# First projection of a sparse-attention layer as seven half-size products, with its bias copies re-queued, and a third row-sum buffer in sample attention

## The reference, cut to what matters

```python
def nsa_project(xn, w_in):                      # xn: tokens x 1024
    p = xn @ w_in                               # 1024 -> 1024 (q) + 6*256 (k/v of three branches) + 48 gates
    q  = p[..., :1024];  kv = p[..., 1024:2560]
    gates = sigmoid(p[..., 2560:])

def compress(x, w1, w2, pe):                    # per 32-row block, stride 16, over cached rows and new ones
    hid = einsum('id,ide->e', pe, w1) + sum_j einsum('nbigd,ide->nbge', xs[:, j:j + nc], w1r[j])
    return silu(hid) @ w2

def nsa_sample(...):                            # for each of the 8 sample sequences
    past = cache_kv[page_table]                 # paged rows, 4 pages of 128 per sequence
    kc, vc = compress(...)                      # compressed keys and values
    # three masked softmaxes with a relative bias: over compressed blocks, over selected
    # blocks, and over a window of 512; outputs are weighted by the gates and summed
```

## Time and profile before

| | |
|---|---|
| median of 3 executions | 2386.98 us (2385.87 to 2387.09) |
| the profiled execution: its own time | 2385.12 us |
| its span in the profile | 2383.4 us |
| TensorE busy | 2283.0 us (96% of the span) |
| VectorE, ScalarE, GpSimd busy | 1062.1, 565.0, 1114.8 us |
| moved by DMA | 197.14 MB, 83 GB/s on average |

### The profile page before, as it was taken

The page is one execution under the profiler, slowest core; times in us unless marked ns, Lnnn a source line. Parts: engine busy times, 40 slices in busy tenths (PEclk is TensorE's granted clock), DMA queues, the critical chain, the costliest instruction groups (busy, mean ns, idle before and its releaser), DMA issues. The chain is left out here.

```text
span 2383.4 us, 37660 instructions
## 1 busy us (share of the span) xinstructions
PE 2283.0 (96%) x14910; PEld 1705.0 (72%) x14910; DVE 1062.1 (45%) x1959; ACT 565.0 (24%) x1303; POOL 1114.8 (47%) x1004
## 2 busy tenths in 40 slices
PE   9999999889999999999999999999999999999997
PEld 7775444466777777767777778687776767777776
DVE  2112786445430242267986646463543153302422
ACT  1002666311000000136554323232420010000011
POOL 3331554255663465375665242342425466634653
PEclk9999999999999999999999999999999999999999
DMA  9723000742211222212222020110203112112211
GB/s 341 238 79 131 1 1 1 238 157 71 71 71 71 88 79 81 107 67 73 61 69 72 6 107 2 57 57 23 90 6 145 72 71 71 71 71 89 89 71 40
DMA packets 53144, 197.14 MB, mean 83 GB/s; under 512 B 15410, under 2 KB 26418, under 8 KB 36978
## 3 DMA queue, kind: packets, MB, share of 16 engines
q1 hardware_dynamic: 45778, 173.59, 20.3%
q0 software_dynamic: 3856, 15.61, 1.9%
q10 hardware_dynamic: 3344, 5.61, 1.1%
HBM read 170.86 MB, written 32.17 MB: 85 GB/s over the span
## 5 line engine op out<-in xcount | busy, mean ns | idle before, releaser
L1803 PE MATMUL ps<-xn,ring 128*128 128x288 f32 x768 | 198.9, 408 | 5.4 <-DVE xn L1906 3.2
L1803 PE MATMUL ps<-hid,ring 128*128 128x288 f32 x768 | 192.8, 406 | 0.0
L1803 PEld LDWEIGHTS ps<-xn,ring 128*128 128x128 f32 x768 | 145.6, 190 | 48.0 <-DVE xn L1906 5.9
L1803 PEld LDWEIGHTS ps<-hid,ring 128*128 128x128 f32 x768 | 145.9, 190 | 40.4 <-ACT p L1840 0.7
L1886 POOL TENSOR_TENSOR prod<-prod,rstd 128x1152 f32<-128x1152 f32 x32 | 83.8, 2620 | 179.7 <-DVE prod L1970 163.4
L1840 ACT ACTIVATE p<-ps 128x288 f32<-128x288 f32 x48 | 19.7, 410 | 597.4 <-PE ps L1803 597.4
L245 PE MATMUL ps<-xn,ring 128*128 128x288 f32 x576 | 140.1, 407 | 1.8 <-DMA ring<-in_w_nsa_in 1.8
L3215 PE MATMUL ps<-xn,ring 128*128 128x288 f32 x512 | 137.1, 415 | 3.6 <-PE ps L3284 3.6
L862 POOL TENSOR_SCALAR ring<-ring,fac 128x128 f32<-128x128 f32 (+2 forms) x96 | 92.6, 981 | 96.1 <-DVE fac L1098 96.1
L1803 PE MATMUL ps<-x_sum,wsum 128*128 128x288 f32 x512 | 130.6, 407 | 3.4 <-DVE x_sum L1910 1.9
L245 PEld LDWEIGHTS ps<-xn,ring 128*128 128x128 f32 x576 | 109.6, 190 | 32.2 <-DMA ring<-in_w_nsa_in 2.3
(11 more groups left out here) (503 smaller groups left out, 4800.8 us busy)
## 6 DMA issues: line engine op xcount, KB each, us to landing
ring<-in_w_mlp SPq DMA_DIRECT2D x64, 1024.0 KB, 4.8
ring<-in_w_gdn_in SPq DMA_DIRECT2D x16, 1024.0 KB, 4.8
ring<-in_w_nsa_in SPq DMA_DIRECT2D x9, 1024.0 KB, 15.8
ring<-in_w_gdn_z SPq DMA_DIRECT2D x8, 1024.0 KB, 4.9
x<-in_seq_state SPq DMA_DIRECT2D x4, 2048.0 KB, 8.4
out_seq_state<-x SPq DMA_DIRECT2D x4, 2048.0 KB, 10.9
ring<-in_w_gdn_out SPq DMA_DIRECT2D x8, 1024.0 KB, 5.7
out_win_old<-in_win_rows POOLq DMA_DIRECT2D x1, 8064.0 KB, 47.7
```

Source lines behind the costliest of these rows:

```text
L1803: mm = nc.tensor.matmul(S.ps[:, base + BANK[p], 0:HT], stationary(p, blk.units[pair // 4], pair % 4), moving(blk.kind, p, pair), start=pai ...
```

## The change

- Units 1 to 9 of the first projection are multiplied as seven products of half size. A unit is laid out as four quarters (`quadrants` instead of `units` in the host's preparation), each of 4 tiles; with the sums of weight quarters (`sum_weights`, 4 VectorE operations of 128x512 a unit) and of token blocks (`sums`, 4 of 128x1152 once) a unit takes 7 x 4 = 28 matmuls of the same shape in place of 32. ScalarE copies three products out of PSUM (`p1`, `p5`, `p6`) and one quarter of the result, VectorE makes the rest (`combine`, 5 operations of 128x288), and `project` scales as before, now in place in `S.qkv`. Unit 0 is multiplied as before (`first_unit`).
- The bias copies go out on SyncE's queue: `near_scratch` in four pieces behind the refills of units 4 to 7, `rows_scratch` in two behind units 8 and 9. They are read back only after the projection, since `toep` and `rowb` hold sums until then. The load of `w2` moves ahead of the refills.
- The token sums lie in the buffer of page set `u` = 2. So GpSimd loads sets 0 and 1 during the projection, and set 2 is loaded after it by three queues: SyncE one page of four, GpSimd one, ScalarE two.
- TensorE's order after the projection is first(0), first(1), gates, second(0), first(2), the transposes, second(1), first(3), second(2), second(3). The four fillers are gone.
- In the sample attention `rsum` has three buffers, `exp` of `n` waits for `combine` of `n - 3`, and the three fillers at `w == 4` are gone.

```diff
-            for u in (0, 2, 1):
-                if u == 2:
+            for u in range(2):
+                if u == 1:
                     pool.wait_ge(setup.summed, 1)
...
+            pool.wait_ge(d.product, 7 * (NB - 1))
+            late_pages(pool, 2, (1,), early_rows[1])
             pool.wait_ge(product, 2)
-            late_pages(pool, 1)
+            late_pages(pool, 3, (1, 3), late[1])
...
+            for n in range(1, NB):
+                base = 4 * (n % 2)
+                pe.wait_ge(d.loaded[n % SLOTS], 16 * (n // SLOTS + 1))
+                for p in PRODUCTS:
...
+                    if p == 2:
+                        pe.wait_ge(p1_read, n)
+                    elif p == 7:
+                        pe.wait_ge(p6_read, n)
+                    elif p == 3:
+                        pe.wait_ge(p5_read, n)
+                    if p in SUMMED:
+                        pe.wait_ge(w_summed, 4 * (n - 1) + SUMMED[p])
...
+                    for pair in range(4):
+                        mm = nc.tensor.matmul(S.ps[:, base + BANK[p], 0:HT], stationary(p, n, pair), moving7(p, pair),
+                                              start=pair == 0 and p in OPENS, stop=pair == 3, skip_group_check=True)
+                    mm.then_inc(d.product, 1)
...
+            def sum_weights(n):
+                slot, s2 = n % SLOTS, n % 2
+                dve.wait_ge(d.loaded[slot], 16 * (n // SLOTS + 1))
+                if n > 2:
+                    dve.wait_ge(d.product, 7 * (n - 2))
+                v.tensor_tensor(wsum[:, s2, 0], quad[:, slot, 2], quad[:, slot, 3], ALU.add).then_inc(w_summed, 1)
+                v.tensor_tensor(quad[:, slot, 2], quad[:, slot, 0], quad[:, slot, 2], ALU.subtract).then_inc(w_summed, 1)
...
+            project(0)
+            project(1)
+            for n in range(1, NB):
+                if n + 1 < NB:
+                    sum_weights(n + 1)
+                combine(n)
...
-        nmax, rsum, fac = sb("dnmax", [128, 2]), sb("drsum", [128, 2, 2]), sb("dfac", [128, 2])
+        nmax, rsum, fac = sb("dnmax", [128, 2]), sb("drsum", [128, 3, 2]), sb("dfac", [128, 2])
...
-                if w == 4:
-                    keep_busy(S, 3, TB)
...
-                if n >= 2:
-                    act.wait_ge(comb, n - 1)
+                if n >= 3:
+                    act.wait_ge(comb, n - 2)
                 a_.activation(sc[w % 3][:], sc[w % 3][:], ACT.Exp, bias=nmax[:, w % 2:w % 2 + 1],
-                              accum_out=rsum[:, n % 2, br:br + 1]).then_inc(prob, 1)
+                              accum_out=rsum[:, n % 3, br:br + 1]).then_inc(prob, 1)
```

More of the change, by code:

```diff
@@ L204, in dense_products @@
     iters = d.units // body
[L206 to L221, removed]
     def group(it, g):
-        if first_in is not None and it == 0 and g == 0:
-            return first_group()
         for ks in range(d.kslots):
@@ L262, in dense_products, with first_unit @@
         group(iters, g)
+def first_unit(pe, S, moving, scaled, first_in, first_mm):
+    nc = S.nc
+    for k in range(KD):
+        pe.wait_ge(*first_in[k // 2])
+        pe.wait_ge(scaled[k % 2], k // 2 + 1)
+        for m in range(2):
+            w = S.ring[:, 0, k * 256 + m * 128:k * 256 + m * 128 + 128]
+            x = moving(k)
+            for half in range(2):
+                mm = nc.tensor.matmul(S.pairs[:, m, half, :], w, x[:, half * HT:half * HT + HT], start=k == 0, stop=k == KD - 1)
+            if k == KD - 1:
+                mm.then_inc(first_mm, 1)
 def dense_chunks(eng, S, d, emit, after=None, ready=None):
@@ L468, in setup_vector @@
                 add_square(j)
+    sums(0)
     dve.wait_ge(u.line_mm, 1)
@@ new lines, in _ @@
+            setup_vector(dve, S, setup, sq, sums)
+            def project(c):
+                out = chunk(S.qkv, c)
+                raw = out
+                if c < 2:
+                    dve.wait_ge(first_mm, c + 1)
+                    raw = S.pairs[:, c]
+                v.scalar_tensor_tensor(out=out, in0=raw, scalar=DH ** -0.5 if c < 8 else 1.0,
+                                       in1=S.rstd[:, 1].rearrange("p (h t) -> p h t", h=2), op0=ALU.mult, op1=ALU.mult
+                                       ).then_inc(made, 1)
@@ new lines, in combine @@
+            def combine(n):
+                a, b, c, e = (S.ps[:, 4 * (n % 2) + k, 0:HT] for k in range(4))
+                after = lambda p: dve.wait_ge(d.product, 7 * (n - 1) + STEP[p])
+                dve.wait_ge(p1_read, n)
+                dve.wait_ge(p6_read, n)
+                if n > 1:
+                    dve.wait_ge(c12, n - 1)
+                v.tensor_tensor(u2, p1, p6, ALU.add).then_inc(u2_set, 1)
+                after(7)
+                if n > 1:
+                    dve.wait_ge(c21, n - 1)
+                v.tensor_tensor(u3, p1, b, ALU.add).then_inc(u3_set, 1)
+                dve.wait_ge(u3_set, n)
+                dve.wait_ge(p5_read, n)
+                v.tensor_tensor(prod(n)[:, 1, HT:T], u3, p5, ALU.add).then_inc(c22, 1)
+                after(4)
+                v.tensor_tensor(prod(n)[:, 1, 0:HT], u3, e, ALU.add).then_inc(c21, 1)
+                after(3)
+                dve.wait_ge(u2_set, n)
+                v.tensor_tensor(prod(n)[:, 0, HT:T], u2, c, ALU.add).then_inc(c12, 1)
+                dve.wait_ge(c11, n)
+                dve.wait_ge(c12, n)
+                dve.wait_ge(c21, n)
+                dve.wait_ge(c22, n)
+                project(2 * n)
+                project(2 * n + 1)
```

192 lines of the change are left out of this document (138 added, 54 removed).

## The result

| | before | after |
|---|---|---|
| median | 2387.03 us (2385.87 to 2389.47, 4 runs) | 2442.03 us (2439.54 to 2446.87, 4 runs) |
| ratio | | 1.0232, 95% interval 1.0219 to 1.0246 |
| profiled execution, its span | 2385.12, 2383.4 us | 2443.72, 2442.1 us |
| first compression product | 168.57 us | 231.00 us (forecast 149.0) |
| start of the prompt attention | 222.27 us | 287.44 us (forecast 204.0) |

The change made the kernel 2.3% slower. The forecast was 2359.3 us; what happened is the rival with a chance of 0.05, and more of it than that rival had priced.

The account below looks back on a forecast made before the run. TensorE's work was taken to bound the first projection, a pipeline across engines the sample attention. 18.2 + 9.5 = 27.7 us off the profiled 2385.1 gave 2357.4, as a median 2359.3 us; range 2354.3 to 2373.

Parts of the forecast that it names:

- Products: First projection, units 1 to 9: 13.58 us a unit, VectorE's sums hidden, compression starts at 149.0, 19.6 us less.
- A quarter took 60.3 / 4 = 15.1 us beside the other copies, and should take less alone.: SyncE's queue, units 5 to 9: each bias piece drains within 15.1 us, so refills stay ahead and cost nothing.
- the bias pieces hold up every refill: Rival, SyncE's queue, units 4 to 9: refills every 20.1 us, 2393.2 us, slower by 6; chance 0.05.
- Unit 4's weights: First projection: needed at 67.5 us, expected in time, cost taken as 0 with bounds 0 and 7.8 us.
- the first rival: First projection: unit 4's weights come late all the same, at 75.3 us, giving 2367.1 us; chance 0.14.
- The count by turns: Unit 4's weights: two queues with work instead of three, so a 34 us wait and arrival near 58 us.
- the count by bytes: Unit 4's weights: about 2.4 MB less beside them at 280 GB/s, 8.7 us, so arrival near 66.6 us.
- Behind unit 9: Compression to next stage: page loads bind by 3 us, stage ends at 204.0; 1.4 of the 19.6 us go here.
- The clock's share: Behind unit 9: 1 us added for a lower TensorE clock after 3 us of idleness.
- Sample attention: Exponential no longer waits for combine, loop takes about 6.0 instead of 6.69 us a sequence: 9.5 us less, lower bound 3.4.
- The 2.7 us for the fillers: Sample attention: with the fillers gone the next transposes come 2.7 us sooner, part of the 13.1 us upper bound.

Follow-up runs that it names:

- rows16_win4: Changed kernel with bias pieces cut across rows (all 16 heads each) and win_old's copy in four later parts: 2361.19 us, ratio 0.9888.
- rows16: Changed kernel with each bias piece cut out of the rows (all 16 heads) instead of out of the heads: 2377.25 us, ratio 0.9963.
- before_win4: Kernel before the change with win_old's copy in four parts behind halves of its page sets 0 and 2: 2387.83 us, ratio 1.0010.
- rsum3_alone: Kernel before the change with only the third row-sum buffer in the sample attention, fillers kept: 2382.41 us, ratio 0.9969.
- win4_busy: rows16_win4 with the old kernel's four filler groups put back ahead of the last compression set: 2367.05 us, ratio 0.9910.
- whole_sp: Changed kernel with the near copy as one DMA behind unit 4's weights and the row copy as one behind unit 9's, on SyncE's queue: 2393.95 us, ratio 1.0042.
- win4_strided: rows16_win4 with near pieces of four heads, each piece read from every fourth partition: 2366.85 us, ratio 0.9919.

## Why the prediction was wrong

**Products.** Right. In rows16_win4 the nine units run from 26.59 to 148.81 us, 13.58 us each, with no wait in between: VectorE's sums are hidden.

**"A quarter took 60.3 / 4 = 15.1 us beside the other copies, and should take less alone."** This is the step that failed. I divided a duration by the number of pieces and took the rate over. The whole copy reads 16 partitions, a piece as it was cut reads four neighbouring ones, and drains at 27 GB/s, 29 us. With the 3 to 4 us of the unit behind it a refill comes every 31 us, not every 13.58. The rival "the bias pieces hold up every refill" had place, mechanism and sign (it turns slower over 18.6 us a unit); its 20.1 us should have been 31. It got 0.05 because I had looked at the packets' size and at what ran beside them, but not at which partitions the source lies in.

**Unit 4's weights.** Taken as 0 with bounds of 0 and 7.8: 7.46 us. The upper bound came, and the first rival with it, hidden under the larger loss. The count by turns gave 58 and the count by bytes 66.6; the weights came at 75.0, as late as before with one copy less beside them. Issuing `win_old` in four later parts ends the wait; that it would was not in the prediction.

**Behind unit 9.** Forecast 55.0 us from the first compression product to the next stage; 56.4 in the changed kernel, 56.2 in rows16_win4. The pages of the last set bind as worked out. The clock's share was 1.7 us (9.72 against 8.0), where I had put 1.

**Sample attention.** Forecast 9.5 us less. By the start of its first score products (483.19 in the changed kernel, 421.93 before) to the output projection it is 68.0 against 75.4 us: 7.4 less, in rows16 4.8, alone on the kernel before 5.8 to 6.2. The loop is shorter as said, and its end takes some back. The 2.7 us for the fillers were counted as if nothing stood behind them; no run shows a gain from them.

**Not in the prediction.** The prompt attention is 3.9 us shorter (195.75 against 199.66 us), at a granted clock of 0.99 against 0.96 in this stage. It isn't a gain of the change: with the same TensorE program the stage takes 198.3 us in rows16 and 194.6 in rows16_win4. The gated-delta stage, which the change doesn't touch, is 3.3 us longer; the last section tells of it. In sum: 82 for the waits and their restarts, 1.4 behind unit 9, 2.1 that the sample attention lacks, 3.3, less 3.9: 85 us over the forecast for the profiled execution (2357.4), and 86.3 were measured.

## What to carry to other kernels

Cut a copy out of SBUF so that every piece still reads from as many groups of four partitions as the whole did: across rows, or with a stride over the partitions, not out of a few neighbouring ones. A piece's time is not the whole's time divided by the number of pieces; ask for each which partitions and how many DMA engines it has, and what stands behind it in its queue. And before an engine gets new work, look for a DMA issue on it that blocks: one that cost nothing before (55.7 us on ScalarE) becomes the critical path.

## What the runs showed of the hardware

- A DMA issue can hold its engine for tens of microseconds while the transfers ahead of it drain: 24.9 to 43.5 us on SyncE behind the changed kernel's pieces, 49.4 and 55.7 us on ScalarE behind the whole copy, against 0.34 us for the first refill.
- Four neighbouring partitions gave 27 GB/s with 4 DMA engines and with nearly 16 (share 0.23 and 0.87). Four partitions four apart gave 98 with 4 engines (share 0.27). A high DMA share is therefore no sign of a high rate, and a copy held to 27 GB/s on all engines took the rate from the others too: 27 GB/s in all, where the same copy on 4 engines left room for 141.
- TensorE's time in a stage can shift without any change to the stage or to its program. Over the gated-delta stage (its first product to the next projection's) I found 530.4 to 530.6 us in the kernel before, before_win4 and rsum3_alone, whose TensorE program is the same, and 531.9 to 537.5 in all others. TensorE's idle time there that the trace names "issue" is part of it: 1.9 us in the kernel before, 5.6 in the changed one, 7.2 in win4_busy. The entries of the changed kernel:

```profile
PE ps L3252 <- issue: 2.7, 5, 1.3
PE ps L3263 <- issue: 1.6, 1, 1.6
PE ps L3269 <- issue: 1.3, 1, 1.3
```

The length of TensorE's program does not explain it: in the changed kernel and the nine with its TensorE program the stage takes 532.3 us (whole_sp) to 536.2 (win4_strided), by one profiled execution each. What the stalls are was not tested. So 4 us between two kernels can be this alone, as with win4_strided (536.2 us there, 2366.9 in all) against rows16_win4 (533.7, 2361.2).
